# First two pieces and the step sizes on x times gain, with the norm's scale applied as they are read out

## The reference

```
h = rms_norm(x, mix_pre_g)            # x * rsqrt(mean(x*x) + 1e-6) * gain
proj = h @ w_in
u_glu, z, xbc, dt_raw, gates = columns of proj
v = (val + b1) * sigmoid(gt + b2)     # val, gt: the halves of u_glu
v = causal_depthwise_conv(v, 31 taps) # then layer norm, silu, a product
dt = softplus(dt_raw + dt_bias)       # step sizes of the state space branch
```

## Time and profile before

| | us |
|---|---|
| median of 3 runs | 975.74 (973.48 to 977.5) |
| the profiled execution | 976.11, span 974.3 |
| TensorE busy | 950.0 (98%) |
| VectorE busy | 706.3 (72%) |
| ScalarE busy | 524.5 (54%) |
| mean granted TensorE clock | 0.989 of full |

### The profile page before, as it was taken

How to read it: one execution, slowest core, us unless ns; L and a number is a source line. 1 busy time by engine, 2 the same in 40 slices (tenths; PEclk the granted TensorE clock), 3 DMA queues, 4 the chain that set the end, 5 groups by cost and what they waited for, 6 DMA issues and landing times.

```text
span 974.3 us, 19194 instructions
## 1 busy us (share of the span) xinstructions
PE 950.0 (98%) x7174; PEld 913.9 (94%) x7174; DVE 706.3 (72%) x1275; ACT 524.5 (54%) x862; POOL 14.1 (1%) x24
## 2 busy tenths in 40 slices
PE   7999999999999999989999999999999999999997
PEld 5999999999998988889999999999987999999996
DVE  5799999999998646658666545788705888888433
ACT  5537666777665254547665534477313655656320
POOL 0000000000000000000000000000000000000000
PEclk8999999999999999999999999999999999999999
DMA  7576334554553536427555655155236555555601
GB/s 271 175 242 200 138 119 169 194 177 136 183 173 107 195 120 238 161 75 249 179 188 181 211 191 184 44 187 183 76 129 200 191 187 179 178 188 177 212 0 43
DMA packets 45180, 161.54 MB, mean 166 GB/s; under 512 B 5028, under 2 KB 6216, under 8 KB 45000
## 3 DMA queue, kind: packets, MB, share of 16 engines
q1 hardware_dynamic: 43632, 155.02, 47.6%
q10 hardware_dynamic: 1496, 5.80, 1.6%
HBM read 159.72 MB, written 1.09 MB: 165 GB/s over the span
## 4 chain that ended last, share of the span: by engine, by line
PE 60%; issue 25%; DVE 9%; ACT 4%; DMA 1%; POOL 0%; DVEq 0%; ACTq 0%; POOLq 0%
PE A L367 11%; PE A L368 11%; PE A L369 11%; PE B L592 5%; PE B L367 3%; PE B L369 3%; PE B L368 3%; PE A L380 3%; PE B L743 3%; DVE w_lo L1142 2%; PE B L733 1%; DVE part L1178 1%; ACT dec L869 1%; PE A L502 1%; PE A L573 1%
## 5 line engine op out<-in xcount | busy, mean ns | idle before, releaser
L367 PE MATMUL A<-h_lo,w_hi 128*128 128x256 f32 x1504 | 432.6, 288 | 3.2 <-DVE h_lo L1519 1.5
L368 PE MATMUL A<-h_hi,w_hi 128*128 128x256 f32 x1504 | 426.0, 283 | 0.0
L369 PE MATMUL A<-h_hi,w_lo 128*128 128x256 f32 x1504 | 425.9, 283 | 0.0
L1142 DVE TENSOR_TENSOR w_lo<-raw,w_hi 128x1024 fp32r<-128x1024 f32 x250 | 303.8, 1221 | 104.6 <-ACT w_hi L772 103.5
L772 ACT ACTIVATE w_hi<-raw 128x1024 fp32r<-128x1024 f32 x250 | 261.7, 1053 | 118.0 <-DMA raw<-in_weights_dram 55.2
L367 PEld LDWEIGHTS A<-h_lo,w_hi 128*128 128x128 f32 x1504 | 288.9, 192 | 7.4 <-issue 3.1
L368 PEld LDWEIGHTS A<-h_hi,w_hi 128*128 128x128 f32 x1504 | 289.1, 192 | 0.3
L369 PEld LDWEIGHTS A<-h_hi,w_lo 128*128 128x128 f32 x1504 | 288.8, 192 | 0.0
L369 PE MATMUL B<-hid_hi,w_lo 128*128 (+1 forms) x368 | 104.1, 283 | 0.0
L367 PE MATMUL B<-hid_lo,w_hi 128*128 (+1 forms) x368 | 104.0, 282 | 0.0
L368 PE MATMUL B<-hid_hi,w_hi 128*128 (+1 forms) x368 | 103.1, 280 | 0.0
(11 more groups left out here) (222 smaller groups left out, 1017.5 us busy)
## 6 DMA issues: line engine op xcount, KB each, us to landing
raw<-in_weights_dram SPq DMA_DIRECT2D x290, 512.0 KB, 4.1
csrow<-cs_dram ACTq DMA_DIRECT2D x9, 512.0 KB, 4.3
x<-in_x_dram SPq DMA_DIRECT2D x2, 512.0 KB, 4.9
bd<-in_lru_w_dram ACTq DMA_DIRECT2D x1, 1024.0 KB, 4.9
out_dram<-m_wide SPq DMA_DIRECT2D x8, 128.0 KB, 2.0
par<-in_params_dram SPq DMA_DIRECT2D x1, 391.0 KB, 5.8
cst<-in_consts_dram SPq DMA_DIRECT2D x1, 320.0 KB, 6.1
wdt<-in_w_dt_dram SPq DMA_DIRECT2D x1, 128.0 KB, 7.1
```

The source lines that it names most:

```text
L367: mm(dst, wh, lo, start=first, stop=False, skip_group_check=free)
L368: mm(dst, wh, hi, start=False, stop=False, skip_group_check=free)
L369: return mm(dst, wl, hi, start=False, stop=last, skip_group_check=free)
L1142: V.tensor_tensor(w_lo[:, s, :], raw[:, s, :], w_hi[:, s, :].bitcast(F32), ALU.subtract).then_inc(lo_ready, 1)
```

## The change

- **Order of loads.** SP loads the first half of x, then 24 columns of `par` (the gain and `glu_b`, 128 rows of 96 B, semaphore `gain_loaded`), then the other half of x, pieces 0 and 1, then `cst` and `wdt`, pieces 2 and 3, then the rest of `par` (`par_loaded`).
- **Weighted input.** VectorE first writes x * gain, 8 instructions, into the place where v of each pair will lie. Piece 0, piece 1 and the step sizes' matmuls use it, so they need no scale. The sum of squares over partitions comes in the middle of piece 1, the spreading of the scale behind it.
- **Scale at the reading out.** ScalarE copies the spread scale to SBUF (`rs`, shown as `mean`). VectorE multiplies the results of piece 0 (into `stage2`) and piece 1 (into v) by it, and the step sizes' raw values before their bias.
- **Operand for the rest.** hf, as before, is written behind the scale, for pieces 2 and on. The split of piece 2 in its middle is gone; all eight come in a row, then the low part of piece 4, then the eight low parts of hf.
- **Plain pieces.** 0, 1, 2 and 3 instead of 0, 1, 5 and 9. Pieces 4 to 15 are all split.

```diff
-GLU_NATIVE = (0, 1, 5, 9)
+GLU_NATIVE = (0, 1, 2, 3)
+EARLY_PAR = AT["conv_dw_w"]
 # SP
                 sp_.dma_start(x[:, ks, :], x_in[:, ks, :]).then_inc(x_loaded[half_x], 16)
-            sp_.dma_start(par[:, :], params_in).then_inc(const_loaded, 16)
-            sp_.dma_start(cst[:, :], consts).then_inc(const_loaded, 16)
+                if half_x == 0:
+                    sp_.dma_start(par[:, 0:EARLY_PAR], params_in[:, 0:EARLY_PAR]).then_inc(gain_loaded, 16)
...
                 if p == 1:
+                    sp_.dma_start(cst[:, :], consts).then_inc(const_loaded, 16)
                     sp_.dma_start(wdt[:, :, :], w_dt).then_inc(wdt_loaded, 16)
+                if p == 3:
+                    sp_.dma_start(par[:, EARLY_PAR:], params_in[:, EARLY_PAR:]).then_inc(par_loaded, 16)
 # TensorE
             stay_clocked(A[2][:, :], 14)
-            pe.wait_ge(const_loaded, 32)
-            summed_squares(1)
-            stay_clocked(A[2][:, :], 1)
-            spread_scale(1)
...
-            first_native(GLU0)
+            gained_x = v[:, :, PAD:]
+            native_piece(GLU0, A[0][:, 0:T], gained_x, gained)
+            native_loaded(GLU0 + 1)
+            for k in range(KD):
+                if k == 4:
+                    pe.wait_ge(const_loaded, 16)
+                    summed_squares(1, B[:, 3, :])
+                ins = mm(A[1][:, 0:T], raw[:, GLU0 + 1, k * P:(k + 1) * P], gained_x[:, k, :], start=k == 0,
+                         stop=k == KD - 1)
+            ins.then_inc(pieces_done, 1)
+            spread_scale(1, B[:, 3, :])
+            pe.wait_ge(wdt_loaded, 16)
+            for k in range(KD):
+                ins = mm(B[0:HEADS, 0, 0:T], wdt[:, k, :], gained_x[:, k, :], start=k == 0, stop=k == KD - 1)
+            ins.then_inc(dt_raw_ready, 1)
 # ScalarE
-            for p in range(2, 4):
-                split_hi(p)
             for k in range(KD):
                 act.wait_ge(staged, k + 1)
                 F(h_hi[:, k, :], hf[:, k, :], ACT.Copy).then_inc(stage_hi, 1)
+            act.wait_ge(rstd_ready, 1)
+            F(rs, up1_rstd, ACT.Copy).then_inc(first_scale, 1)
             for p in range(4, LEAD):
                 split_hi(p)
...
-                act.wait_ge(pieces_done, p + 1)
+                if c == 0:
+                    act.wait_ge(first_scaled, 1)
+                else:
+                    act.wait_ge(pieces_done, p + 1)
 # VectorE
+            for c in range(KD):
+                dve.wait_ge(x_loaded[c // (KD // 2)], 16)
+                V.tensor_scalar(v[:, c, PAD:], x[:, c, :], col("mix_pre_g", c), None, ALU.mult).then_inc(gained, 1)
             sum_squares(acc, 0)
...
-                V.scalar_tensor_tensor(hf[:, k, :], x[:, k, :], col("mix_pre_g", k), rstd, ALU.mult,
+                V.scalar_tensor_tensor(hf[:, k, :], x[:, k, :], col("mix_pre_g", k), up1_rstd, ALU.mult,
                                        ALU.mult).then_inc(staged, 1)
-                if k == 3:
-                    split_lo(2)
+            split_lo(GLU0 + 4)
             for k in range(KD):
                 operand_low(k, hf[:, k, :], h_hi[:, k, :], h_lo[:, k, :])
-            for p in range(3, LEAD):
-                split_lo(p)
-
+            dve.wait_ge(first_scale, 1)
+            dve.wait_ge(dt_raw_ready, 1)
+            V.tensor_tensor(stage2[:, 0, :], A[0][:, 0:T], rs, ALU.mult).then_inc(first_scaled, 1)
+            first_value = own.up(V.tensor_tensor(v[:, 0, PAD:], A[1][:, 0:T], rs, ALU.mult))
+            split_lo(GLU0 + 5)
```

More of the change, by code:

```diff
@@ L281, in hybrid_kernel @@
         const_loaded, wdt_loaded = sem("const_loaded"), sem("wdt_loaded")
+        gain_loaded, gained, first_scaled = sem("gain_loaded"), sem("gained"), sem("first_scaled")
+        par_loaded, first_scale = sem("par_loaded"), sem("first_scale")
         hi_ready, lo_ready, pieces_done = sem("hi_ready"), sem("lo_ready"), sem("pieces_done")
@@ L489, in _ @@
             stay_clocked(A[2][:, :], 14)
-            pe.wait_ge(const_loaded, 32)
-            summed_squares(1)
-            stay_clocked(A[2][:, :], 1)
-            spread_scale(1)
[L495 to L505, removed]
-            first_native(GLU0)
-            for c in range(KD):
-                for j in range(2 if c else 0):
+            gained_x = v[:, :, PAD:]
[13 more added lines that the diff above has]
+            ins.then_inc(dt_raw_ready, 1)
+            for c in range(1, KD):
+                for j in range(2):
                     if c >= 2:
@@ L513, in _ @@
                     if p in NATIVE:
-                        native_piece(p, dst, hf)
+                        native_piece(p, dst, hf, staged if j == 0 else None)
                     else:
[L516 to L522, removed]
+                        chunk_piece(p, 0, dst, h_hi, h_lo, 0 if p == GLU0 + 4 else None)
             def step_transposes():
@@ L790, in _ @@
             dtw = gates
-            act.wait_ge(const_loaded, 32)
+            act.wait_ge(gain_loaded, 16)
+            act.wait_ge(par_loaded, 16)
             for c in range(KD):
@@ L795, in _ @@
                 split_hi(p + LEAD)
-                act.wait_ge(pieces_done, p + 1)
+                if c == 0:
+                    act.wait_ge(first_scaled, 1)
+                else:
+                    act.wait_ge(pieces_done, p + 1)
                 if c >= 2:
                     act.wait_ge(pairs_drained, c - 1)
-                F(stage2[:, c % 2, :], A[2 * (c % 2)][:, 0:T], ACT.Sigmoid,
+                F(stage2[:, c % 2, :], A[2 * (c % 2)][:, 0:T] if c else stage2[:, 0, :], ACT.Sigmoid,
                   bias=col("glu_b", KD + c)).then_inc(gate_ready, 1)
@@ L1209, in sum_squares @@
                 add_squares_up()
+            dve.wait_ge(constants_written, 4)
+            dve.wait_ge(gain_loaded, 16)
+            for c in range(KD):
+                dve.wait_ge(x_loaded[c // (KD // 2)], 16)
+                V.tensor_scalar(v[:, c, PAD:], x[:, c, :], col("mix_pre_g", c), None, ALU.mult).then_inc(gained, 1)
             sum_squares(acc, 0)
[L1213 to L1216, removed]
+            moment_of(1, D, RMS_EPS, up1_sums).then_inc(mean_ready, 1)
             dve.wait_ge(rstd_ready, 1)
             for k in range(KD):
-                V.scalar_tensor_tensor(hf[:, k, :], x[:, k, :], col("mix_pre_g", k), rstd, ALU.mult,
+                V.scalar_tensor_tensor(hf[:, k, :], x[:, k, :], col("mix_pre_g", k), up1_rstd, ALU.mult,
                                        ALU.mult).then_inc(staged, 1)
-                if k == 3:
-                    split_lo(2)
+            split_lo(GLU0 + 4)
             for k in range(KD):
                 operand_low(k, hf[:, k, :], h_hi[:, k, :], h_lo[:, k, :])
-            for p in range(3, LEAD):
-                split_lo(p)
+            dve.wait_ge(first_scale, 1)
[3 more added lines that the diff above has]
+            split_lo(GLU0 + 5)
             def log1p_first(e, t1, t2, t3, t4):
@@ L1253, in step_sizes @@
                     dve.wait_ge(dt_raw_ready, 1)
-                    after(own.up(V.tensor_scalar(dw[3], B[0:HEADS, 0, 0:T],
+                    after(own.up(V.tensor_tensor(dw[4], B[0:HEADS, 0, 0:T], rs[0:HEADS, :], ALU.mult)))
+                    after(own.up(V.tensor_scalar(dw[3], dw[4],
                                                  par[0:HEADS, AT["dt_bias"]:AT["dt_bias"] + 1], None, ALU.add)))
@@ L1279, in _ @@
             GLU_TAPS, LOOP_TAPS, LATE_TAPS = range(5), range(5, CONV_K - 4), range(CONV_K - 4, CONV_K)
-            dve.wait_ge(constants_written, 4)
+            dve.wait_ge(const_loaded, 16)
+            dve.wait_ge(par_loaded, 16)
             for c in range(KD):
@@ L1284, in _ @@
                 dve.wait_ge(gate_ready, c + 1)
-                V.scalar_tensor_tensor(v[:, c, PAD:], A[2 * (c % 2) + 1][:, 0:T], col("glu_b", c), stage2[:, c % 2, :],
-                                       ALU.add, ALU.mult).then_inc(pairs_drained, 1)
+                if c == 0:
+                    after(first_value)
+                V.scalar_tensor_tensor(v[:, c, PAD:], A[2 * (c % 2) + 1][:, 0:T] if c else v[:, 0, PAD:], col("glu_b", c),
+                                       stage2[:, c % 2, :], ALU.add, ALU.mult).then_inc(pairs_drained, 1)
                 dve.wait_ge(pairs_drained, c + 1)
```

## The result

| | before | changed |
|---|---|---|
| median of 6 runs, us | 974.48 (973.11 to 977.50) | 978.10 (974.90 to 980.82) |
| the profiled execution, us | 976.11 (span 974.3) | 978.19 (span 976.4) |
| mean granted clock | 0.989 | 0.993 |

The ratio is 1.0038, 95% interval 1.0021 to 1.0054: the changed kernel is slower by 2.0 to 5.3 us, within the 0.5% that the forecast called no change. So the direction of the shift held, and 978.10 lies in the range of 973.4 to 979.6, but the size of the shift didn't hold.

A forecast was written before the change was run, and what follows sets the result against it. VectorE's chain was taken to bound the opening, TensorE the group loop. Later operand start 4.5, wait 1.75 and added work 1.1, less 6.7 idle, gave +0.7 us, 976.4 us forecast; range 973.4 to 979.6.

The forecast's parts named there:

- The bound of the opening: Opening up to 75 us: VectorE's chain to v of pair 5 decides; TensorE being ready earlier has no effect alone.
- T: Start of the normalised operand on VectorE, forecast at 16.2 us, 4.5 us later than the old 11.66.
- the waits before pieces 4, 10, 12 and 14: TensorE waiting for v: 26.3 to 27.4 us, then about 2.6, 1.9 and 1.5 us, spending its earlier start.
- The first rival: Opening: VectorE isn't the bound, TensorE's head start comes through, piece 14 starts 7 us earlier, 969 us; chance 0.08.
- The wait for ScalarE: VectorE's first split, of piece 4, waits 1.75 us for ScalarE's high part; bounds 1.0 and 2.2 us.
- the idle time removed: VectorE's waits before v of pairs 0, 1 and 2 and before the first split go, 6.7 us.
- the added work: VectorE before v of pair 2: two scalings and one for the step sizes, 1.1 us; bounds 0.8 and 1.5.
- The load term: Gain's 12 KB load between x and piece 0: cost taken as 0, upper bound 1.0 us; piece 0 at 7.8 us.
- Rival 2: The clock falls at piece 14 or in pieces 0 and 1, costing 1.7 us, 978.1 us; chance 0.24.
- the rule I weighed: Bursts parted by waits start cold: TensorE's three new waits each cost 1.7 us on top of 0.7, 981.5 us.
- rival 3: Clock low throughout pieces 0 and 1: twelve matmuls cost 5.25 us more, 981.7 us; chance 0.06.

The follow-up runs named there:

- the load third: Changed kernel with the gain's 12 KB load behind both halves of x in SP's queue, not between them: 974.25 us, 0.9996 of the kernel before.
- the load moved: Changed kernel with the gain's load on ScalarE's queue (974.57 us, 1.0001 of the kernel before) or behind both x halves in SP's queue (974.25 us, 0.9996).
- the best version: Changed kernel with early sums, pieces 0 to 3, 5 and 9 plain, gain's load on ScalarE's queue, 20 zeros: 970.15 us, 0.9958 of the kernel before.

## Why the prediction was right and wrong

**The bound of the opening: right.** VectorE's chain from T on decides, and TensorE's head start is spent in waits for v; the constant 45.52 us, the waits before pieces 4, 10, 12 and 14, and the run with ScalarE's splits first show it. The first rival (the head start comes through) is out: in the changed kernel TensorE was ready 1.24 us early for piece 14 and it gained nothing.

**The terms behind T: right.** The wait for ScalarE 1.70 (1.75), the idle time removed, the added work about 1.0 (1.1): with T at 16.10 as in the run with the load third, v of pair 2 came at 38.27 (38.8 said) and v of pair 5 at 61.62, 0.0 us from before, where +0.7 was said. T, the wait and the added work make 0.3 of the 0.5 us at pair 2; the rest shows on no single row.

**The load term: mis-sized, and that is the miss.** I wrote of the 12 KB between x's halves "from below it costs nothing; from above 1.0 us" and took 0. In the two profiles of the changed kernel it cost 0.9 and 2.0 us in the landing of x's second half (7.4 and 8.5 against 6.5) and 0.8 and 1.9 in the start of piece 0 (8.81 and 9.93 against 7.99 with the load third), so up to twice the bound: I had priced the bytes of the load and not its effect on those behind it, for which no row stood. Of the delay of x, 0.4 us is SP's later issue, which is no byte of the load either. T went from the forecast 16.2 (measured 16.1 without it) to 16.9 and 19.7.

**Rival 2 came on top in some executions.** The profile of the changed kernel had the low clock in pieces 0 and 1, for 1.7 us, all in T; the second profile had not. A later piece 0 lengthens the idle time behind the zeros. Four profiles have the load between the halves and 14 zeros. The two where TensorE idled 2.59 and 2.96 us had the low clock behind that, the two with 1.16 and 1.26 had not; with the load moved, neither profile had it (1.75 and 0.75). So the late load can bring the low clock with it. The five executions of 18 that took over 980 us fit this, but no trace of them shows it. The waits before pieces 10 and 12 cost nothing, as said, which also speaks against the rule I weighed: of its three payments one fell due, and the next wait covered it (the two profiles with the load moved show that, piece 12 starting at 54.89 and 54.90). The slower side (rival 3) didn't come to pass: even the profile with the longest low clock, that of the kernel with rows of 512 B, lost 3.1 us in the 12 matmuls, not 5.25. Single executions of the changed kernel did reach 980.0 to 981.5, but the median didn't; the interval ends at 0.54%.

The sum of the two is 0.8 us of T in one profile and 3.6 in the other; the medians show 3.6 us (2.0 to 5.3) and, with the load moved, -0.4 (-1.5 to 0.7).

**The bounds were added wrongly.** The terms give 976.4 - 0.75 - 0.3 = 975.35 and 976.4 + 0.45 + 0.4 + 1.0 = 978.25, not 975.2 to 977.8. The measured 978.10 lies inside the right sum and outside the written one, and that is luck. The forecast stood on 975.74 for the kernel before, and beside the changed kernel that measured 974.48. The shift of 3.6 us on the base as taken would be 979.3, outside both sums and just inside the range of 979.6.

What stays open is why a load between x's halves slows the loads behind it. It is not rows under 512 B (rows of 512 B did the same), not its presence in the queue ahead of piece 0 (third, it cost nothing), and not the pieces. 12 KB and 64 KB did alike; other sizes, or a small load between two large ones elsewhere in the queue, weren't tried.

## What to carry to other kernels

When a stage has two full engines, find the wait that ends it and follow the other engine's chain back to its start: work moved ahead of the start of that chain costs its full time, however much idle time it fills on the first engine. A reordering of loads is to be judged by the landings of all that stand behind, read from a profile of that order, not by bytes over bandwidth. And before an opening is rebuilt, fill TensorE's idle time ahead of it with zeros: here that alone gave 2.4 us (1.3 to 3.5).

## What the runs showed of the hardware

- One load of 12 or 64 KB between two of 512 KB in the same queue lowered the core's rate from 4 to 8 us to between 258 and 309 GB/s in seven profiled executions; in seven without it, it was 365 to 409.
- In the profile of the best version the granted clock was full until 960 of 967 us, and its span ended 910.2 us behind v of pair 5; in the kernel before, with three stretches of lowered clock behind 300 us, it was 912.7. Which executions have them is decided by more than the code: the changed kernel had one of them in its first profile and two in its second. Over all fourteen profiled executions the part behind v of pair 5 took 910.2 to 913.2 us, with nothing changed there.
